# Eight scan turns written out, and the first expert group's gathers spread between the first expert's products, with four weight slots loaded a block earlier

## What is computed

```
h = rms_norm(x, norm_mix_g) * (1 + scale_m) + shift_m
proj = h @ w_in                                   # SSD columns and RWKV columns
y_ssd  = ssd_mixer(proj[..., :N_SSD_IN], ...)     # 16 heads, forward and backward
y_rwkv = rwkv7_mixer(proj[..., N_SSD_IN:], ...)   # 16 heads, forward and backward
x = x + gate_m * (concat(y_ssd, y_rwkv) @ w_out)
h = rms_norm(x, norm_ffn_g) * (1 + scale_f) + shift_f
aff = softmax(h @ router_w); gate, idx = top_k(aff.T, cap)      # expert choice, 16 experts
hid = silu(xs @ w_gate[e]) * (xs @ w_up[e]);  out = hid @ w_down[e] * gate
x = x + gate_f * scatter_add(out);  y = rms_norm(x, final_norm_g)
```

## Time and profile before

| what | us |
|---|---|
| median of 3 runs | 2522.35 (2521.81 to 2524.38) |
| the profiled execution, its own time | 2528.3 |
| its span, first to last instruction | 2526.7 |
| PE busy in the span | 2205.4 (87%) |
| DVE busy | 853.0 (34%) |
| mean granted clock of TensorE | 0.953 |
| bytes moved | 594.10 MB, mean 235 GB/s |

### The profile page before, as it was taken

How to read it: one execution, slowest core, us unless ns; L and a number is a source line. 1 busy time by engine, 2 the same in 40 slices (tenths; PEclk the granted TensorE clock), 3 DMA queues, 4 the chain that set the end, 5 groups by cost and what they waited for, 6 DMA issues and landing times. The chain is left out here.

```text
span 2526.7 us, 38426 instructions
## 1 busy us (share of the span) xinstructions
PE 2205.4 (87%) x16156; PEld 1124.0 (44%) x16156; DVE 853.0 (34%) x1816; ACT 393.3 (16%) x788; POOL 154.4 (6%) x185
## 2 busy tenths in 40 slices
PE   6785999989998898988987997988988998889886
PEld 2243555445665555656655554322422332243222
DVE  2161344434455454555553103111221221122123
ACT  1112122212321222222210111000100010010002
POOL 0000111100010010010110110000000000000000
PEclk9897999999999999989998998999999999999999
DMA  9924899932111111111101319999999999999996
GB/s 367 342 51 153 294 337 340 319 102 61 48 37 30 46 31 37 36 38 36 41 27 42 104 50 374 413 413 413 413 413 413 413 413 413 413 413 413 413 413 278
DMA packets 271138, 594.10 MB, mean 235 GB/s; under 512 B 25869, under 2 KB 166247, under 8 KB 249863
## 3 DMA queue, kind: packets, MB, share of 16 engines
q1 hardware_dynamic: 253575, 524.64, 55.5%
q0 software_dynamic: 17408, 67.11, 7.0%
HBM read 586.89 MB, written 4.82 MB: 234 GB/s over the span
## 5 line engine op out<-in xcount | busy, mean ns | idle before, releaser
L1804 PE MATMUL bank<-arena,picked 128*64 128x512 f32 x1280 | 302.9, 618 | 49.8 <-DMA arena<-exp_w_up 47.0
L1074 PE MATMUL bank<-arena,w_rkv 128*128 128x384 f32 x768 | 289.3, 516 | 1.6 <-ACT raw_rkv L1264 1.5
L1983 DVE TENSOR_TENSOR x_sum<-x_sum,bank 128x512 f32<-128x512 f32 x180 | 115.5, 684 | 326.5 <-PE bank L1789 326.5
L1804 PEld LDWEIGHTS bank<-arena,picked 128*64 128x64 f32 x1280 | 97.9, 141 | 246.2 <-issue 245.5
L1828 PE MATMUL bank<-w_exp,hid 128*64 128x512 f32 x768 | 176.7, 597 | 6.9 <-DMA w_exp<-exp_w_down 6.7
L1804 PE MATMUL bank<-w_exp,picked 128*64 128x512 f32 x768 | 174.9, 597 | 8.8 <-DMA w_exp<-exp_w_up 8.5
L1074 PEld LDWEIGHTS bank<-arena,w_rkv 128*128 128x128 f32 x768 | 141.2, 196 | 91.9 <-issue 19.1
L690 PE MATMUL bank<-arena,w_xz 128*128 128x384 f32 x448 | 157.4, 499 | 15.9 <-DMA w_xz<-w_in 15.9
L690 PEld LDWEIGHTS bank<-arena,w_xz 128*128 128x128 f32 x448 | 82.1, 191 | 96.4 <-issue 29.9
L1870 ACT COPY gu<-bank 112x512 f32<-112x512 f32 x32 | 17.2, 589 | 691.3 <-PE bank L1804 691.3
L1048 POOL TENSOR_TENSOR WI<-WX,cst 128x384 f32<-128x384 f32 x80 | 78.6, 999 | 732.1 <-DVE WX L1465 502.0
(11 more groups left out here) (370 smaller groups left out, 2676.0 us busy)
## 6 DMA issues: line engine op xcount, KB each, us to landing
w_exp<-exp_w_down SPq DMA_DIRECT2D x96, 1024.0 KB, 20.9
arena<-exp_w_gate SPq DMA_DIRECT2D x80, 1024.0 KB, 19.0
arena<-exp_w_up SPq DMA_DIRECT2D x80, 1024.0 KB, 19.2
w_ada<-w_ada POOLq DMA_DIRECT2D x64, 1024.0 KB, 8.0
w_exp<-exp_w_gate SPq DMA_DIRECT2D x48, 1024.0 KB, 18.5
w_exp<-exp_w_up SPq DMA_DIRECT2D x48, 1024.0 KB, 18.5
w_ada<-w_ada SPq DMA_DIRECT2D x32, 1024.0 KB, 17.9
arena<-exp_w_down SPq DMA_DIRECT2D x32, 1024.0 KB, 18.3
```

The lines of the kernel that those rows point to most:

```text
L1074: mm = pe.matmul(ps[6][:, 0:T], w[:, m % 3, n % 8], hT[:, n % KC], start=(n % KC == 0), stop=(n % KC == KC - 1))
L1804: mm = pe.matmul(ps[b][COLS[j], :], picked[:, k, at:at + 64], halves[j][:, c * 1024 + b * 512:c * 1024 + (b + 1) * 512], start=(k == 0), s ...
L1983: V.tensor_tensor(y, y if e else x, ps[(LAST_BANKS[i // 2 % 4] if e == LAST else 6) + i % 2][:], ALU.add).then_inc(S("added"), 1)
```

## The change

1. In `rwkv` the loop of pairs 1 to 5 on SP, PE, ACT and DVE, and the loop of 8 pairs on POOL, are written out: every pair has instructions of its own, with constant addresses and counts.
2. A new tile `w_early` of 4 slots (4 MB in all) holds slots 0 to 3 of the ring. They are loaded at the end of `project_out`'s SP queue, and SP waits for them before that block ends. In `experts` SP skips these four; the ring still has 12 slots: 4 of `w_early`, 6 in `arena`, 2 of its own.
3. `pick(0)` is cut up. PE does k = 0 and 1 ahead of `up(0)`; in step kk of `up(0)` it does picks 2kk+2 and 2kk+3, then waits for the eviction of picks 2kk and 2kk+1 alone, then does the step's products. As products now use banks 0 and 1 meanwhile, the first group's context picks go to banks 4 and 5.

```diff
         def turns(eng, body):
-            body(0, False, 2)
-            with eng.Fori(1, PAIRS - 2) as p:
-                body(p, True, 2)
-            body(PAIRS - 2, True, 1)
-            body(PAIRS - 1, True, 0)
+            for p in range(PAIRS):
+                body(p, p > 0, min(PAIRS - 1 - p, 2))
...
-            with pool.Fori(0, PAIRS) as p:
+            for p in range(PAIRS):
                 for n in range(1, 6):
...
+            block = expert_rows(I)
+            for n in range(EARLY):
+                sp.dma_start(w_early[:, n].rearrange("p (c n) -> p c n", c=2), block(0, n)).then_inc(S("early_loaded"), 16)
             sp.wait_ge(S("gfin_loaded"), 16)
+            sp.wait_ge(S("early_loaded"), 16 * EARLY)
...
-        w = [arena[:, n * 2048:(n + 1) * 2048] for n in range(HOME)] + [more[:, n] for n in range(RING - HOME)]
+        w = [w_early[:, n] for n in range(EARLY)] + [arena[:, n * 2048:(n + 1) * 2048] for n in range(HOME)] + [more[:, n] for n in range(RING - HOME - EARLY)]
...
                     g = e * NS + n
+                    if g < EARLY:
+                        continue
...
-            def pick(g):
+            def pick(g, k0=0, k1=KC):
+                bank = 0 if g else 4
...
-                for k in range(KC):
+                for k in range(k0, k1):
...
             def up(e):
-                if e == 0 or e in PICK_AT:
-                    pe.wait_ge(S("picked_c"), KC * (PICK_AT.get(e, 0) + 1))
-                    pe.wait_ge(S("picked_s"), KC * (PICK_AT.get(e, 0) + 1))
+                if e in PICK_AT:
+                    pe.wait_ge(S("picked_c"), KC * (PICK_AT[e] + 1))
+                    pe.wait_ge(S("picked_s"), KC * (PICK_AT[e] + 1))
                 at = e % PACK * SLOTS
                 for kk in range(8):
+                    if e == 0:
+                        if kk < 7:
+                            pick(0, 2 * kk + 2, 2 * kk + 4)
+                        pe.wait_ge(S("picked_c"), 2 * kk + 2)
+                        pe.wait_ge(S("picked_s"), 2 * kk + 2)
...
             route()
-            pick(0)
+            pick(0, 0, 2)
```

More of the change, by code:

```diff
@@ L166, in program @@
             acc = sb(ffn, "x_sum", [P, KC * T])
+            w_early = sb(ffn, "w_early", [P, EARLY, 2048])
             late = dict(gates=sb(ffn, "gates", [P, D // 2]), gfin=sb(ffn, "gfin", [P, D]), shifts=sb(ffn, "shifts", [P, 48]),
-                        acc=acc, sums=acc[:, 0:T], logits=acc[0:48, T:2 * T], xtok=xtok)
+                        w_early=w_early, acc=acc, sums=acc[:, 0:T], logits=acc[0:48, T:2 * T], xtok=xtok)
             project_out(**env, mixed=mixed, **late)
@@ L1533, in _, with expert_rows, block, project_out @@
             end(PAIRS - 1)
-def project_out(nc, I, O, table, S, sb, ps, cst, par, modT, gain, xT, C, mixed, gates, gfin, acc, sums, logits, shifts, xtok):
+EARLY = 4
+def expert_rows(I):
+    wide = [I[n].rearrange("l e (q c p) n -> p (l e q) c n", p=P, c=2) for n in ("exp_w_gate", "exp_w_up")]
+    tall = I["exp_w_down"].rearrange("l e (q p) n -> p (l e q) n", p=P)
+    def block(e, n):
+        return wide[n % 2][:, e * 8 + n // 2] if n < 16 else tall[:, e * 8 + n - 16]
+    return block
+def project_out(nc, I, O, table, S, sb, ps, cst, par, modT, gain, xT, C, mixed, gates, gfin, w_early, acc, sums, logits, shifts, xtok):
     RING, BANKS = 4, 3
@@ L1666, with experts @@
 PACK = 4
-def experts(nc, I, O, table, S, sb, ps, cst, par, modT, gain, xT, C, arena, gates, gfin, acc, sums, logits, shifts, xtok):
+def experts(nc, I, O, table, S, sb, ps, cst, par, modT, gain, xT, C, arena, gates, gfin, w_early, acc, sums, logits, shifts, xtok):
     HOME = 2 * KC * T // 2048
@@ L1680, in experts @@
     PICK_AT = {PACK * g: g for g in range(1, PACKS)}
-    wide = [I[n].rearrange("l e (q c p) n -> p (l e q) c n", p=P, c=2) for n in ("exp_w_gate", "exp_w_up")]
-    tall = I["exp_w_down"].rearrange("l e (q p) n -> p (l e q) n", p=P)
+    rows = expert_rows(I)
     with ExitStack() as st:
-        more = sb(st, "w_exp", [P, RING - HOME, 2048])
-        w = [arena[:, n * 2048:(n + 1) * 2048] for n in range(HOME)] + [more[:, n] for n in range(RING - HOME)]
+        more = sb(st, "w_exp", [P, RING - HOME - EARLY, 2048])
+        w = [w_early[:, n] for n in range(EARLY)] + [arena[:, n * 2048:(n + 1) * 2048] for n in range(HOME)] + [more[:, n] for n in range(RING - HOME - EARLY)]
         picked = sb(st, "picked", [P, KC, PACK * SLOTS + PAD])
@@ L1718, in _ @@
                     g = e * NS + n
+                    if g < EARLY:
+                        continue
                     if g >= RING:
                         sp.wait_ge(S("exp_used"), g - RING + 1)
[L1721 to L1725, removed]
+                    dst = w[g % RING].rearrange("p (c n) -> p c n", c=2) if n < UPS else w[g % RING]
+                    sp.dma_start(dst, rows(e, n)).then_inc(loaded[g % RING], 16)
             for i in range(TILES * 4):
@@ L1736, in arrived @@
                 g = e * NS + n
-                pe.wait_ge(loaded[g % RING], (g // RING + 1) * 16)
+                if g >= EARLY:
+                    pe.wait_ge(loaded[g % RING], (g // RING + (g % RING >= EARLY)) * 16)
                 return w[g % RING]
@@ L1754, in route @@
                 mm.then_inc(S("rank_T"), 1)
-            def pick(g):
[L1758 to L1761, removed]
-                for k in range(KC):
+            def pick(g, k0=0, k1=KC):
+                bank = 0 if g else 4
+                if k0 == 0:
+                    pe.wait_ge(S("onehot"), min(g, 1) + 1)
+                    if g:
+                        pe.wait_ge(S("gu_out"), 2 * PACK * g)
+                        pe.wait_ge(S("G"), PACK * g)
+                for k in range(k0, k1):
                     i = KC * g + k
@@ L1766, in pick @@
                         pe.wait_ge(S("picked_s"), i - 1)
-                    pe.matmul(ps[k % 2][:, 0:PACK * CAPC], xtok0(k), ohc[:, PACK * g:PACK * (g + 1)].rearrange("p e c -> p (e c)"), start=True, stop=True).then_inc(S("pick_c"), 1)
+                    pe.matmul(ps[bank + k % 2][:, 0:PACK * CAPC], xtok0(k), ohc[:, PACK * g:PACK * (g + 1)].rearrange("p e c -> p (e c)"), start=True, stop=True).then_inc(S("pick_c"), 1)
                     for t in range(2):
@@ L1964, in pick @@
                     V.tensor_scalar(picked[:, k, 0:PACK * SLOTS].rearrange("p (e s) -> p e s", s=SLOTS)[:, :, 0:CAPC],
-                                    ps[k % 2][:, 0:PACK * CAPC].rearrange("p (e c) -> p e c", e=PACK), gain[:, 1, k, 1:2], modT[:, 3 * KC + k, 1:2],
+                                    ps[(0 if g else 4) + k % 2][:, 0:PACK * CAPC].rearrange("p (e c) -> p e c", e=PACK), gain[:, 1, k, 1:2], modT[:, 3 * KC + k, 1:2],
                                     ALU.mult, ALU.add).then_inc(S("picked_c"), 1)
```

## The result

The change made the kernel faster: a median of 2487.35 us (2484.22 to 2490.25, 4 runs) against 2522.57 for the kernel before beside it, ratio 0.9859 (95% interval 0.9842 to 0.9876). That is 35.2 us; the forecast was 35.4 and 2487.

A forecast was written before the change was run, and what follows sets the result against it. PE bounds the pairs, transfers the experts. Pairs 18.25 + 5.0 + 2.0 = 25.3 us, plus experts 10.1, make 35.4 off the median 2522.35: 2487 us. Range 2474 to 2499, about 0.8.

The forecast's parts named there:

- Rival A: Whole kernel: the forecast itself, both the pairs and the experts pay, 2487 us; chance 0.70.
- The four gaps: Pairs: PE's four idle "issue" brackets at the loop's head vanish with nothing in their place, 18.25 us.
- D: Pairs: "issue" gaps come back elsewhere in straight code and only the experts pay, 2512 us; chance 0.05.
- Cold starts and clock: Pairs 2 to 5: slow starts at a lowered clock after each gap go; half counted, 5.0 us, ends 0 and 9.9.
- Rival B: Pairs: the cold starts' saving returns as longer cold stretches behind `gate`; about 15 of 25.3 us stay, 2497; chance 0.09.
- E: Pairs: the clock stays up all through, 25 us in five pairs where 5 are counted, 2467 us; chance 0.06.
- Constants on DVE: Pairs: constant counts save DVE 0.41 us a pair ahead of `gate`, 2.0 us over five, ends 0 and 5.
- Early slots alone 0, picks alone 3.3, first reload 10.1 sooner: Experts: early slots alone gain nothing, spread picks alone only the 3.3 us pause; together the first reload moves 10.1 us.
- Is the stream then fed?: Experts, `up(0)`: a step of 5.05 us frees two slots that take 5.08 to fill; no loss, ends 0 and about 10.
- rival C: Experts: a thin queue, interleaved steps pay a restart each and the 10 us are lost, 2497; chance 0.07.
- What is late next: Pairs: once the gaps go, PE's wait for the bonus ahead of L1108 is late next, and it stays.
- rival F: Pairs: slower, from fetching five more pairs' instructions, 40 packets; at twice 0.89 us a packet, 2558 us; chance 0.03.

The follow-up runs named there:

- the repeat: The changed kernel itself, unaltered, timed again in a later call; 2488.43 us, 0.9860 of the kernel before.
- e6_pe_straight: The changed kernel with the pair loop put back on SP, ACT and DVE, PE and POOL written out; 2497.86 us, 0.9897 of the kernel before.
- e2: The kernel before with the four early slots and the spread picks, pair loops kept; 2517.09 us, 0.9981 of the kernel before.
- e4: The kernel before with the spread picks only, no early slots, pair loops kept; 2517.68 us, 0.9979 of the kernel before.
- e9_ssd_straight: The changed kernel with the loops over the head groups of `ssd` written out as well; 2482.58 us, 0.9830 of the kernel before.
- e1_pairs_only: The kernel before with only the pair loops of `rwkv` written out on every engine; 2494.53 us, 0.9892 of the kernel before.
- e5_pe_looped: The changed kernel with the loop of pairs 1 to 5 put back on PE alone; 2514.68 us, 0.9956 of the kernel before.
- e12_one_way_back: The changed kernel with pairs 1 and 2 as a loop on PE alone; 2494.36 us, 0.9893 of the kernel before.

## Why the prediction was right, and which terms were not

Rival A held, and both halves paid. The sum came out to a fraction of a microsecond, but that is luck: terms off in opposite directions met.

**The four gaps, 18.25: the mechanism right, the size that of one execution.** The brackets vanish in straight code and come back with PE's own loop alone, or once with one way back. But they last 3.1 to 5.0 us each, with one or two instruction packets in them: before's profile had 18.3 in all, the other looped ones 13.0, 14.8, 15.0 and 14.4. On average the term is nearer 15. D is ruled out: no pair in straight code has such a bracket.

**Cold starts and clock, 5.0: too small.** PE's busy time for the same products fell 18.3 us between the profiles (434.92 to 416.65, clock 0.95 to 0.99), and pairs 1 and 5 ran in 89.85 us, pair 1 at a mean clock of 1.00. With only PE looped its busy time is back at 429.70 (clock 0.96), and pairs 1 to 5 take 480.7 us against 455.3 to 460.1 in the five profiles of kernels that are straight on every engine and keep `gate` where it was (mean 457.3); of the difference of 23.4, 14.4 are brackets, so 9 hang on what follows a way back. PE's busy time is 11.1 us over the mean of those five (418.6; they lie between 416.6 and 421.5), and its idle time only 12.3 over theirs, so some 2 us of the brackets come back as shorter waits. I had seen 9.9 there and halved it because pair 6's clock also falls; the halving was the error. The 467 us named for pairs 1 to 5 were undershot by 7 to 12.

```profile
685.53:1166.23 480.70, 429.70 (x5882) 292.46 (x5880) 249.82 (x496) 119.65 (x235) 48.98 (x50) 0.96 0.15 38
```

Rival B is refuted, and E was nearly met in pairs 1 to 5, but not behind them: pairs 6 and 7 took 190.7 before, 186.3 after and 195.3 in the repeat, with 2345 or 2346 products each time and the clock between 0.97 and 0.92:

```profile
1144.05:1330.30 186.25, 166.06 (x2345) 114.55 (x2344) 95.99 (x201) 35.81 (x70) 19.60 (x20) 0.97 0.11 29
```

```profile
1143.89:1339.20 195.31, 175.13 (x2346) 119.45 (x2344) 96.01 (x201) 35.71 (x70) 19.61 (x20) 0.92 0.10 28
```

**Constants on DVE, 2.0 with ends 0 and 5: near as a wait, too small with what the clock adds.** `e6_pe_straight`, where SP, ACT and DVE keep the loop, takes 464.0 us, 6.7 over the mean. Its idle time explains 464.02 - 422.44 - 38.7 = 2.9 of that, and that is clear: the five straight profiles have 38.6 to 38.9 us of idle time. The other 3.8 are PE busy longer at clock 0.98; the five differ by 4.9 among themselves there, so one profile can't settle that part.

```profile
684.99:1149.01 464.02, 422.44 (x5882) 290.12 (x5880) 249.27 (x496) 118.94 (x235) 49.03 (x50) 0.98 0.15 39
```

The loops' two costs add up in the profiles: 23.4 + 6.7 = 30.1, and the three looped profiles of `e2` to `e4` lie 487.1 - 457.3 = 29.8 above the straight ones.

Why then do the medians give the pairs 27 us and not 30? In part the stretch from the last pair to the first load of `experts` is longer, by 2.3 us here and about as much in most kernels with straight pairs, though not in `e6_pe_straight` and `e9_ssd_straight`. It isn't the early loads: `e1_pairs_only` has it without them. The timeline places it at the first products of `project_out`, first of before, then of after: PE waits 0.8 us longer for the first `w_out` load, and the 16 products behind it take 1.45 us longer.

```profile
1384.45 6.99 PE L1596 MATMUL bank<-arena,w_out_ring 128*128 128x384 f32 x16 [11.55 <-DMA w_out_ring<-w_out]
```

```profile
1346.36 8.44 PE L1612 MATMUL bank<-arena,w_out_ring 128*128 128x384 f32 x16 [12.35 <-DMA w_out_ring<-w_out]
```

Why that load comes later stays open, and so does the last microsecond or two, which the intervals cover.

**Early slots alone 0, picks alone 3.3, first reload 10.1 sooner:** measured 0, 4 to 5, and 10.65. SP was not late at the barrier.

**"Is the stream then fed? ... Taken at no loss": this is the step that failed**, with 10.1 forecast and 7.5 measured in the stage. The step took 5.12 us where 5.05 was reckoned, more than the 5.08 that two slots need, so the one pair ahead could not grow; and at the end of `up(0)` and in `turn`, where PE is busy 2.61 of 5 us, the rate fell. That is rival C's loss in small, without a restart at every step. That the queue starves there is not shown: a thirteenth slot left the dips as they were, and in them the rate falls further than the share of busy DMA engines (0.99 at 386 GB/s and, with 13 slots, 0.99 at 347, against 1.02 at 413), so part of the loss is packets that take longer. What slows them stays open; it needs early slots and spread picks together. The stream's end says how much it cost. The last packets came 2501.5 - 1516.48 = 985.0 us after the first load before and 2456.7 - 1479.86 = 976.8 after, 8.2 less, where four slots fewer make 10.2. So 2.0 us more were lost on the way: the pause cost 3.5 in place of 4.0 ((413 - 309) x 5 / 413 + (413 - 299) x 10 / 413, from the windows of before below), the dips 1.6, and 0.9 I could not place. What follows the last packet took 25.8 us in place of 25.2.

```profile
1545.00:1550.00 5.00, 4.41 (x28) 2.57 (x28) 4.11 (x15) 1.43 (x4) 0.00 (x0) 1.00 0.77 309
1550.00:1560.00 10.00, 10.00 (x50) 4.08 (x48) 0.10 (x1) 0.00 (x0) 0.00 (x0) 1.00 0.78 299
...
2501.50:2502.00 0.50, 0.05 (x2) 0.05 (x2) 0.00 (x0) 0.00 (x0) 0.00 (x0) 1.00 0.00 0
```

```profile
2456.70:2457.20 0.50, 0.01 (x2) 0.01 (x2) 0.00 (x0) 0.00 (x0) 0.00 (x0) 1.00 0.00 0
```

**What is late next,** the wait for the bonus, was right: moving `gate` one half-level gave some 18 us by the medians, more than the 14.3 of the wait. PE's idle time in pairs 1 to 5 fell by 5.4 of that; how much the clock gave isn't shown.

**The fetch, rival F:** 122 packets on q8 in place of 131 and 30 on q14 in place of 24, with fewer instructions in all, and nothing took the brackets' place: PE's idle time in pairs 1 to 5 fell by 18.5 us where the brackets had been 18.3. The loop did not save fetches: over pairs 1 to 5 before moved 56 packets on q8 and 2 on q14, after 47 and 9. The rule quoted from the Trainium skill ("Runtime: NRT & Kernel Launch", "Instruction fetch mechanics"), that a taken branch to a target that is not held makes work wait, fits `e5_pe_looped` and `e12_one_way_back`, one bracket for each way back with one or two instruction packets in it.

## What to carry to other kernels

Bytes moved ahead of a stream that never stops need not shorten it by their transfer time: here four slots, 10.2 us, gave nothing alone and some 3 us beside the spread picks. Compare the step that frees slots with the time those slots take to fill, and when the two are within some per cent of each other, count a loss; why it arises was not shown here. An idle bracket ended by "issue" at a loop's head is worth writing out; look there for packets of the instruction queue. The clock that PE gains by not stopping can be worth nearly as much as the gap itself. One profiled execution gives the mechanism, not the size: the same four gaps of the same loop were 13 us in one execution and 18 in another, so read them in several before they go into a sum.

## What the runs showed that was not expected

The way back cost PE 3.1 to 5.0 us in a body of 1176 products, with one or two instruction packets in the gap, and nothing measurable in one of 182, which is 99% busy and moves none. A straight pair's length falls into groups: in the kernel after, pairs 1 to 5 took 89.85, 91.38, 91.46, 91.45 and 89.85 us with the same code, and the two windows below, of pairs 1 and 2, differ by 83.65 - 82.11 = 1.54 us of busy PE with the clock at 1.00 and 0.98.

```profile
688.73:778.58 89.85, 82.11 (x1176) 56.59 (x1175) 49.69 (x99) 23.99 (x47) 9.80 (x10) 1.00 0.15 39
778.84:870.22 91.38, 83.65 (x1176) 57.57 (x1174) 49.79 (x99) 23.99 (x47) 9.80 (x10) 0.98 0.15 39
```
